# A joined two-block transformer kernel: half-width products in the recurrence levels, a rebuilt entry into the memory attention, and the pooling branch on another engine

## The reference

```
for l in range(DEPTH):
    h = _rms(x, mix_norm_g[l])
    x = x + (_even_mixer if l % 2 == 0 else _odd_mixer)(h, ...)
    x = x + _memory_cross_attention(_rms(x, xa_norm_g[l]), _rms(mem, xa_mem_norm_g[l]), ...)
    x = x + _conv_ffn(_rms(x, ffn_norm_g[l]), ...)
```

```
q = _rms(_split_heads(h @ w_q, XA_HEADS), q_norm_g)
mk, mv = _split_cols(mem_h @ w_kv, (XA_HEADS * XA_HD, XA_HEADS * XA_HD))
mk = _rms(_split_heads(mk, XA_HEADS), k_norm_g)
logits = jnp.einsum('bhqd,bhkd->bhqk', q, mk) * (XA_HD ** -0.5)
p = jax.nn.softmax(logits, axis=-1)
o = jnp.einsum('bhqk,bhkd->bhqd', p, mv)
```

```
lagged = jnp.pad(csg[:, :S - w], ((0, 0), (w, 0), (0, 0)))
counts = jnp.minimum(t + 1.0, float(w))[None, :, None]
groups.append((csg - lagged) / counts - uf[:, :, sl])
```

## Time and profile before

| what | value |
| --- | --- |
| time, median of 3 runs | 3182.88 us (3181.28 to 3187.20) |
| time of the profiled execution | 3179.84 us |
| its span, first to last instruction | 3178.0 us |
| mean granted TensorE clock, share of full speed | 0.992 |
| PE busy | 3118.1 us (98%) |
| DVE busy | 1584.6 us (50%) |
| ACT busy | 1076.7 us (34%) |
| POOL busy | 281.8 us (9%) |

### The profile page before, as it was taken

The page is one execution under the profiler, slowest core; times in us unless marked ns, Lnnn a source line. Parts: engine busy times, 40 slices in busy tenths (PEclk is TensorE's granted clock), DMA queues, the critical chain, the costliest instruction groups (busy, mean ns, idle before and its releaser), DMA issues.

```text
span 3178.0 us, 38774 instructions
## 1 busy us (share of the span) xinstructions
PE 3118.1 (98%) x15548; PEld 2603.7 (82%) x15548; DVE 1584.6 (50%) x1852; ACT 1076.7 (34%) x1167; POOL 281.8 (9%) x161
## 2 busy tenths in 40 slices
PE   9999999999999899999999999999999999999998
PEld 7798988888889798888888778888888777888887
DVE  7574545554325554455435754544334765444433
ACT  3223334443223443444323332333322332233322
POOL 0002100110000020010001200111000200100100
PEclk9999999999999999999999999999999999999999
DMA  4411412222321131222233122222222222222223
GB/s 168 112 54 67 146 40 93 92 100 104 123 97 67 42 145 54 80 94 104 94 110 109 54 93 93 93 96 100 95 106 92 90 74 100 93 93 96 99 103 112
DMA packets 47721, 299.92 MB, mean 94 GB/s; under 512 B 7091, under 2 KB 7347, under 8 KB 13284
## 3 DMA queue, kind: packets, MB, share of 16 engines
q1 hardware_dynamic: 42480, 288.01, 25.7%
q10 hardware_dynamic: 5108, 10.02, 1.4%
HBM read 293.26 MB, written 4.75 MB: 94 GB/s over the span
## 4 chain that ended last, share of the span: by engine, by line
PE 90%; DVE 5%; ACT 2%; issue 2%; DMA 0%; POOL 0%; DVEq 0%; ACTq 0%; SPq 0%
PE G L443 82%; ACT wH L1197 1%; DVE wL L1614 1%; PE psS L782 1%; DVE mxt L1821 1%; PE psS L503 1%; PE psS L982 1%; PE G L989 1%; DVE ws L2336 1%; PE psS L1080 1%; PE G L1089 1%; DVE ws L2333 0%; PE psT L535 0%; PE psT L1116 0%; PE G L1007 0%
## 5 line engine op out<-in xcount | busy, mean ns | idle before, releaser
L443 PE MATMUL G<-hH,wH 128*128 128x512 f32 x2560 | 1019.9, 398 | 20.4 <-DVE ws L2364 5.7
L443 PE MATMUL G<-hH,wL 128*128 128x512 f32 x2560 | 1001.9, 391 | 0.0
L443 PE MATMUL G<-hL,wH 128*128 128x512 f32 x2560 | 1001.0, 391 | 0.0
L1614 DVE TENSOR_TENSOR wL<-raw,wH 128x2048 fp32r<-128x2048 f32 x265 | 637.5, 2406 | 647.3 <-ACT wH L1197 646.9
L443 PE MATMUL G<-wsr,wH 128*128 128x512 f32 (+1 forms) x2528 | 750.7, 380 | 1.4 <-DVE wsr L2202 0.9
L1197 ACT ACTIVATE wH<-raw 128x2048 fp32r<-128x2048 f32 x265 | 505.5, 1908 | 587.7 <-PE G L443 567.8
L443 PEld LDWEIGHTS G<-hH,wH 128*128 128x128 f32 x2560 | 483.6, 189 | 136.8 <-issue 17.6
L443 PEld LDWEIGHTS G<-hH,wL 128*128 128x128 f32 x2560 | 482.9, 189 | 103.2
L443 PEld LDWEIGHTS G<-hL,wH 128*128 128x128 f32 x2560 | 483.7, 189 | 99.5 <-issue 2.2
L443 PEld LDWEIGHTS G<-wsr,wH 128*128 128x128 f32 x2528 | 466.2, 189 | 94.8 <-DVE wsr L2202 1.8
L443 PE MATMUL G<-wsr,wL 128*128 128x512 f32 (+1 forms) x1264 | 479.0, 379 | 0.0
(11 more groups left out here) (275 smaller groups left out, 2570.2 us busy)
## 6 DMA issues: line engine op xcount, KB each, us to landing
raw<-in_units SPq DMA_DIRECT2D x265, 1024.0 KB, 4.8
ws<-bias_rows SPq DMA_DIRECT2D x2, 1536.0 KB, 14.9
bias_rows<-ws ACTq DMA_DIRECT2D x1, 2560.0 KB
x<-in_x SPq DMA_DIRECT2D x4, 512.0 KB, 7.4
ws<-in_mem ACTq DMA_DIRECT2D x2, 1024.0 KB, 5.0
ws<-bias_rows ACTq DMA_DIRECT2D x1, 2048.0 KB, 8.2
out_x<-x SPq DMA_DIRECT2D x4, 512.0 KB, 7.9
ws<-in_decay ACTq DMA_DIRECT2D x1, 1280.0 KB, 8.0
```

The lines of the kernel that those rows point to most:

```text
L443: mm = pe.matmul(o, mv if swap else wt, wt if swap else mv, start=first and n == 0, stop=last and n == 2)
L1614: V.tensor_tensor(wL[:, g.p, :], raw[:, g.p, :], wH[:, g.p, :].bitcast(F32), ALU.subtract)\
```

## The change

In levels 1 to 5 PE multiplies only the query columns of the later halves (64 instead of 128 in each product) into 256 columns of `psS`, and DVE copies only those. The transfers of the memory are issued earlier, in the middle of the mixers. The squared sums of the queries of the memory attention are made, read and raised to the power per job instead of all at once, and part of the work of the fourth query job (its read, the key scaling, the split of the next unit, on ACT and DVE) moves into the first five rows of the attention. ACT runs one exponential on a scratch column before the fourth query job. In the second block the squared sum of the later queries moves from `fill(10)` to `fill(13)` and into another PSUM bank, and the pooling branch moves from POOL to DVE, spread over `fill(17)` to `fill(27)`, with its rounding rest in the gate jobs behind the attention. Counter constants follow.

The diff, cut to its core:

```diff
+            def attention(rows, nk, probs, score, pv, per_job, scores_read, l, keys_read):
 
 
                 pe.wait_ge(kv_ready, c.lay.v + 1)
 
-                pe.wait_ge(ms_ready, c.stat.v)
-
+                pe.wait_ge(ms_ready, keys_read + 2)
...
                     if s_ < rows:
+                        if s_ == 12:
+                            pe.wait_ge(last_ready, l + 1)
+                            pe.wait_ge(job_free, last_query)
 
                         wait(pe, scores_read, c.row.v + (s_ - 1))
                         score(s_).then_inc(s_done, 1)
+                    if s_ == 1:
+                        stats("pair", 3, st=G[:, c.job.p * 2 + 1, :])
...
                         pe.wait_ge(pt_ready, c.row.v + (r + 1))
+                        if r == 0:
+                            pe.wait_ge(ms_ready, keys_read + 4)
...
                             for o, ks, qs, w in parts:
-                                mm = pe.matmul(psS[:, n % 2, o:o + w], k_[:, ks:ks + P], q_[:, qs:qs + w],
-                                               start=True, stop=True)
+                                q = q_[:, qs:qs + w]
+                                if 0 < lev < 6:
+                                    o, w, q = o // 2, w // 2, blocks(q, 2 ** (lev + 1))[1]
+                                mm = pe.matmul(psS[:, n % 2, o:o + w], k_[:, ks:ks + P], q, start=True, stop=True)
...
                     if j:
-                        stats("pair", j - 1, added=7 * l + 4 + j)
+                        pe.wait_ge(ms_ready, c.stat.v)
+                        stats("pair", j - 1, npairs=j, st=st if j < 3 else G[:, c.job.p * 2, :],
+                              added=7 * l + 4 + j)
                 c.nrm.off += 8
-                stats("pair", 3)
...
-                    elif s_ == 10:
-
+                    elif s_ == 9:
+                        key_norm()
+                    elif s_ == 11:
                         pe.wait_ge(kn_read, (c.lay.v - 2) * 2 - 1)
-                        stats("half", 0, npairs=1, st=G[:, 3, :])
-                    elif s_ in (9, 11):
                         key_norm()
+                    elif s_ == 13:
+
+                        pe.wait_ge(pv_free, c.pv.v + 1)
+                        stats("half", 0, npairs=1, st=G[:, 1, :])
...
-                            pe.wait_ge(pv_free, c.pv.v + 1)
+                            pe.wait_ge(ms_ready, c.stat.v)
...
                 if mem is not None:
-                    act.dma_start(memt[mem], a["mem"]).then_inc(mem_in, 16)
...
-                    if between and s_ == rows - LAG:
+                    if between and s_ == 3:
...
                         ins.then_inc(hc_ready, 1)
+                    act.dma_start(memt[0], a["mem"]).then_inc(mem_in, 16)
                     step()
                     in_place(GG + 2, ACT.Silu)
...
+                        elif s_ == 20:
+                            act.dma_start(memt[1], a["mem"]).then_inc(mem_in, 16)
...
                 for j in range(4):
-                    step(square)
+                    step(square, unit=j < 3)
+                    if j == 2:
+                        activation(tick[:, 2 + l:3 + l], neghalf[:], ACT.Exp)
...
+                                    later = lambda t: t.rearrange("p k (n two l) -> p k n two l", two=2,
+                                                                  l=2 ** (lev + 1))[:, :, :, 1, :]
+                                    b = psS[:, n % 2, 0:256].rearrange("p (k n l) -> p k n l", k=4, l=2 ** (lev + 1))
+                                    d = later(ws[:, DD + h, :].rearrange("p (k q) -> p k q", q=P))
+                                    mask = later(hmask[:, lev:lev + 1, :].bitcast(I32).to_broadcast([P, 4, P]))
                                     wait(dve, hm_ready, n - 3)
-                                    ins = V.copy_predicated(d, hmask[:, lev:lev + 1, :].bitcast(I32)
-                                                            .to_broadcast([P, 4, P]), b)
+                                    ins = V.copy_predicated(d, mask, b)
...
+                def queries(j):
+                    def read(g):
                         for t in range(2):
                             ins = V.tensor_scalar(ws[:, XQ + 2 * j + t, :], g[:, t, :],
                                                   gqk[:, 1 + 2 * l + t:2 + 2 * l + t], None, ALU.mult)
                         ins.then_inc(job_free, 1)
-                    step(squared(j, queries))
-                    if j < 3:
-                        add_pair(j, S)
-                    dve.wait_ge(rb_ready, c.bc.v - (1 if j < 3 else 0))
-                    ins = V.tensor_tensor(kx[:, 2 * j:2 * j + 2, :], kx[:, 2 * j:2 * j + 2, :],
-                                          psT[:, (first + j) % 2, 0:M].unsqueeze(1).to_broadcast([P, 2, M]), ALU.mult)
+                    return squared(j, read)
+                def key_scale(j):
+                    return V.tensor_tensor(kx[:, 2 * j:2 * j + 2, :], kx[:, 2 * j:2 * j + 2, :],
+                                           psT[:, (first + j) % 2, 0:M].unsqueeze(1).to_broadcast([P, 2, M]), ALU.mult)
+                def query_norm(j):
+                    dve.wait_ge(sq_used, c.sq.v + j + 1)
+                    at = st if j < 2 else G[:, pv_slot * 2 + j - 2, :]
+                    V.tensor_scalar(ms[:, 4 * j:4 * j + 4], at[:, 4 * j:4 * j + 4], 1.0 / 256, EPS, ALU.mult, ALU.add)\
+                        .then_inc(ms_ready, 1)
+                    c.stat.off += 1
+                norms = c.stat.v
+                pv_slot = c.job.p
+                for j in range(3):
+                    columns(2 * j + 2, 2)
+                    step(queries(j))
+                    add_pair(j, S)
+                    dve.wait_ge(rb_ready, c.bc.v - 1)
+                    ins = key_scale(j)
+                    if j:
+                        query_norm(j - 1)
                 ins.then_inc(kv_ready, 1)
-                rstd(4, 16, 256)
                 xprobs = lambda r: ws[:, XP + r % 4, 0:M]
                 def row(r):
+                    if r % 4 == 0:
+                        dve.wait_ge(rs_ready, norms + r // 4 + 1)
                     c.link(row_max(r, psS[:, r % 2, 0:M]))
                     V.tensor_tensor(mxt[:, r % 4:r % 4 + 1], mxt[:, r % 4:r % 4 + 1], rsq[:, r:r + 1], ALU.mult)\
                         .then_inc(mx_ready, 1)
+                def between(s_):
+                    if s_ == 0:
+                        dve.wait_ge(rb_ready, c.bc.v)
+                        key_scale(3).then_inc(last_ready, 1)
+                    elif s_ == 1:
+                        query_norm(2)
+                    elif s_ == 2:
+                        step(queries(3), unit=False)
+                    elif s_ == 3:
+                        query_norm(3)
+                    elif s_ == 4:
+                        split()
+                        c.sq.off += 4
...
-                    elif s_ == 11:
-                        rstd_part(G[:, 3, :])
                     elif s_ == 12:
                         half_keys(1)
                         half_scaled(1, PX_)
+                    elif s_ == 15:
                         rstd_part_scaled(rsq[:, 16:32])
+                    elif s_ in (17, 19, 21, 23, 25, 27):
+                        pooled((s_ - 17) // 2)
...
+                def window(dst, src, lag):
+                    c.link(V.tensor_tensor(dst[:, :, lag:S], src[:, :, lag:S], src[:, :, 0:S - lag], ALU.add))
+                    c.link(V.tensor_copy(dst[:, :, 0:lag], src[:, :, 0:lag]))
+                def pooled(n):
+                    if n == 0:
+                        dve.wait_ge(pinv_in, (c.lay.v - 2) * 16)
+                        window(pa, u, 1)
+                    elif n == 1:
+                        window(pb, pa, 2)
+                    elif n == 2:
+                        window(pa[:, 1:2, :], pb[:, 1:2, :], 4)
+                    elif n == 3:
+                        window(pb[:, 1:2, :], pa[:, 1:2, :], 8)
+                    else:
+                        t, rows, widths = ((pa, lo, (2, 8)), (pb, hi, (4, 16)))[n - 4]
+                        start = t[rows, :, 0:16]
+                        c.link(V.tensor_tensor(start, start, ws[rows, PINV:PINV + 2, 0:16], ALU.mult))
+                        V.tensor_tensor(start, start, u[rows, :, 0:16], ALU.subtract)
+                        for i, width in enumerate(widths):
+                            ins = V.scalar_tensor_tensor(t[rows, i, 16:S], t[rows, i, 16:S], 1.0 / width, u[rows, i, 16:S],
+                                                         ALU.mult, ALU.subtract)
+                        ins.then_inc(pd_ready, 1)
+                def pooled_low():
+                    dve.wait_ge(pdh_ready, c.lay.v - 3)
+                    for t, rows in ((pa, lo), (pb, hi)):
+                        ins = V.tensor_tensor(wsr[rows, PL:PL + 2, :], t[rows], wsr[rows, PX_:PX_ + 2, :].bitcast(F32),
```

(59 more changed lines are left out.)

27 lines of the change are left out of this document (11 added, 16 removed).

## The result

Four executions of the changed kernel took 3145.74 to 3153.94 us, median 3152.85, against 3185.04 us for the kernel before on the same chip: ratio 0.9895, 95% interval 0.9877 to 0.9914. Two later sets gave 3147.48 us (0.9886, 0.9871 to 0.9902) and 3150.25 us (0.9901, 0.9885 to 0.9918). The forecast was 3147.0, the range 3134 to 3166.

The account below looks back on a forecast made before the run. PE, busy for 98% of the span, was taken to bound the kernel. The terms 0 + 9.5 + 4.4 + 7.4 + 13.4 = 34.7 us, off the profiled 3179.84, gave 3145.1; the forecast was 3147 us, range 3134 to 3166.

Parts of the forecast that it names:

- What bounds the kernel: Whole kernel: PE bounds it, busy for 98% of the span; losses are 59.9 us of idle PE and 25 us of clock.
- Levels, 0: Levels 1 to 5: halved moving columns gain 0 us, as columns below 128 don't set the rate; bounds 0 and 0.6.
- Memory's transfer, 9.5: Memory's sums, both layers: the earlier transfer removes waits and part of the clock loss, 9.5 us; bounds 4.3 and 12.9.
- Half of the clock loss: Memory's sums: half of the 3.4 + 3.4 us of clock loss goes, 3.4 us, as 4 us of one-column matmuls stay.
- The 1.8 us for the run of 32 records: Memory's one-column sums: waiting for the third and fourth square and the low clock's start go, 0.9 us each, 1.8 us.
- Entry, 4.4: Entry into the memory attention: the changed order gains 2.2 us per layer, 4.4 us for two; bounds 0 and 14.5.
- The 3.0 us per layer: Memory attention: row 7's score starts some 3.0 us earlier than before, taken as the entry's gain per layer before the clock.
- The half clock loss: Entry into the memory attention: half of one 1.7 us clock loss taken off the 3.0 us per layer, leaving 2.2.
- Later queries' squares, 7.4: Second block: PE's 2.0 us wait for DVE's bank read and 1.7 us clock loss go in each layer, 7.4 us.
- Pooling, 13.4: Second block: with POOL silent, 7.3 + 6.1 us of idle PE and clock loss go, DVE's added work covered; bounds 0 and 13.4.
- three signs of being wrong: Pair step below 3 us in the levels; low clocks staying in the eight places; new PE waits on DVE in steps 9 to 14.
- the rival, DVE as the bound: Second block's attention: DVE's 8 us replace the stretching, PE keeps its idle times, the 13.4 go: 3160 us; chance 0.10.

Follow-up runs that it names:

- both64: Changed kernel with 64 moving columns and only the first 64 of 128 stationary columns in levels one to five (scores not the reference's): 3142.67 us.
- stat64: Changed kernel with 128 moving columns but only the first 64 of 128 stationary columns in levels one to five (scores not the reference's): 3157.0 us.

## Why the prediction was right, and where not

**What bounds the kernel: right.** 21.0 us of the 26.1 are idle PE, at the places named.

**Levels, 0: right in size, the reason too narrow.** I took the flat price from 1 to 128 columns as the weight load alone. The shapes fit another rule: a record costs the larger of two terms, one by stationary and one by moving columns, which meet at 128 x 128 for this type at 1.95 / 16 = 0.12 us. It is a fit to these few shapes; the terms are not quite proportional (both64 takes 1.15 us for sixteen, half of 1.95 would be 0.98). By it half the columns alone gain nothing. What was gained, 0.6 us of idle PE behind level 5, is the upper bound that I had given for DVE's shorter copies.
The Trainium skill, page "TensorE: Matmul & The Clock Gate", section "Back-to-back issue gap", also gives some 81 ns for a sustained pair of weight load and matmul at 128 columns; the 0.12 us of these f32 records do not agree. The section "LDWEIGHTS (loading the stationary operand)" on the same page of the Trainium skill gives a time in proportion to the weight columns. In both64 this nearly agrees, where the weight loads of 64 columns take 1.01 us for sixteen against 1.98 for 128 columns; in stat64, with 128 moving columns, the same loads take 1.72 us, so it is not enough for a sum.

**Memory's transfer, 9.5: measured 6.0 (2.9 to 9.2).** The forecast lies just above the interval. The 4.3 us of waiting went. Half of the clock loss was right as a mean: 7.9 us in both layers with the late transfer, 4.4 with the early transfer; in the trace of this run it stayed whole (3.4 us in each layer). The 1.8 us for the run of 32 records was too much: 4.85 us became 4.32 in layer 0 and 4.92 became 4.62 in layer 1, 0.8 us. What is left above the 1.84 us that 16 such records take at clock 1.00 is low clock, which the other term counts already.

**Entry, 4.4: measured 5.1 (1.9 to 8.0).** Right in size, with the term for the clock wrong. The 3.0 us per layer are an earlier start of row 7, taken against starts in the trace before that hold the low clock already; so they contain its going. The half clock loss that I took off again did not stay: the loss went in both layers (10 of 10 to 0 of 18). By the starts, counted from the end of the fourth job's matmuls, row 7 of layer 0 comes 3.8 us earlier in the changed kernel; 0.5 us of that is lost at row 12, so 3.3 are left behind it. Idle time is the smaller part of this: over 40 us from the fourth job on it fell by 1.0 us in layer 0 and 1.3 in layer 1. The simulated stalls were there, at rows 4 to 7, 2.4 us for the 3.4 that I had: DVE's read of 1.40 us and its split of 2.29 hold PE 0.95 and 0.75 us:
```profile
424.31 1.40 DVE L2280 TENSOR_SCALAR ws<-G,gqk 128x512 f32<-128x512 f32 x2
424.68 1.13 PE L994 MATMUL psS<-ws 128*128 128x256 f32 x4 [0.32 <-ACT ws L1501]
426.98 1.13 PE L994 MATMUL psS<-ws 128*128 128x256 f32 x4 [0.95 <-ACT ws L1501]
427.09 1.91 ACT L1212 ACTIVATE wH<-raw 128x2048 fp32r<-128x2048 f32 x1
429.03 2.29 DVE L1633 TENSOR_TENSOR wL<-raw,wH 128x2048 fp32r<-128x2048 f32 x1 [1.28 <-ACT wH L1212]
429.60 1.13 PE L994 MATMUL psS<-ws 128*128 128x256 f32 x4 [0.38 <-ACT ws L1501]
432.60 1.13 PE L994 MATMUL psS<-ws 128*128 128x256 f32 x4 [0.75 <-ACT ws L1501]
```
The waits are put down to ACT, which reads the bank; behind ACT stands DVE's row maximum, behind that the read or the split.

**Later queries' squares, 7.4: measured 8.0 (5.1 to 10.8).** Right in mechanism and size.

**Pooling, 13.4: the step that was mis-sized; measured 7.0 (3.8 to 9.9).** Two causes. The claim that failed is that DVE's new work is covered from step 9 to 13. In step 11, one of the two that I called tightest, DVE comes to the scaled read L2425 behind its two probability scalings and PE waits 0.95 us per layer in the changed kernel. A part of the pooling, 0.9 us, stands in the run of DVE work ahead of it. With the pooling alone PE waits 0.64 us there and 0.28 us some 30 us later, 1.8 us in both layers, of the 10.1 us of idle time before. So two of my three signs of being wrong came in part: a new wait of PE on DVE in steps 9 to 14, and low clocks that stay at two of the eight places, the memory's sums.
```profile
1801.29 0.49 DVE L2523 TENSOR_SCALAR ws<-ws,rden 128x512 f32<-128x512 f32 x1
1801.69 0.68 DVE L2425 TENSOR_TENSOR ws<-G,hmask 128x512 f32<-128x512 f32 x1
1802.43 0.50 PE L443 MATMUL G<-hH,wH 128*128 128x512 f32 x1 [0.95 <-DVE ws L2425]
```
And of the clock losses one moved to the unchanged wait behind (last row of the table), 1.7 us in this run's trace. The two make 3.5 us of the 6.4 by which the term was too large; the rest lies inside the interval and has no cause found. So the rival, DVE as the bound, was true for some 2 us of its 13.4.

**The sum.** The five parts alone make 6.0 + 7.0 + 8.0 + 5.1 - 1.3 = 24.8 us, each with some 3 us of uncertainty, thus about 7 on the sum; I had added 34.7, and the whole change measured 33.4, 36.3 and 31.5. The total is thus nearer than the terms were, two of which were too large by 3.5 and 6.4 us, and that is in part luck. That the parts gain more together than apart is suggested by the clock losses (24.0 us before, 18.8 to 41.0 with one part, 8.6 to 17.0 with all) and not shown. The miss of the first set, 5.9 us above the forecast, goes with the clock: within the set the granted mean went from 0.994 (3153.73 us) to 0.998 (3145.74 us), and the profiled execution has 8.4 us of clock loss at four places (204, 1040, 1064 and 2616 us) where the trace before has none.

## What to carry to other kernels

Before you halve an operand, find which side sets the price of a record: in this f32 stream with a new weight load for each product, 64 moving columns cost what 128 do (1.89 and 1.95 us for sixteen), and only both sides together gain (1.15). Count a clock loss to a wait only with a probability: it may go, stay (as at a long run of one-column sums) or move on to the next wait. And cut long pieces of side work to the slack of one row before you put them between rows; here that took PE's waits from 5.5 to 1.6 us, while a gain in time was not shown.

## What was not expected of the hardware

The same program had 17.0, 12.0 and 8.6 us of low clock in three executions, in steps of 1.7 us, with the same waits. A wait of 1.86 us that never brought a low clock in ten cases brought one in 13 of 18 after waits some 40 to 110 us ahead of it had been removed, in kernels where DVE has POOL's work. And sixteen records with 64 stationary and 128 moving columns took 1.96 us, as long as full ones, though the same weight loads of 64 columns take 1.01 us for sixteen beside 64 moving columns, against 1.98 for 128; the step from pair to pair even grew, from 3.17 to 3.47 us.
